# Inverting the 16x16 diagonal blocks of the recurrent chunks elementwise on VectorE, by way of DRAM, in place of eight TensorE products per pair of heads; the end of the group norm moved into the chain

## The reference, cut to what matters

```
def step(state, inp):
    r_t, w_t, k_t, v_t, aa_t, bb_t = inp
    sa = jnp.einsum('bhvk,bhk->bhv', state, aa_t)
    state = state * w_t[:, :, None, :] + sa[..., None] * bb_t[:, :, None, :] + v_t[..., None] * k_t[:, :, None, :]
    return state, jnp.einsum('bhvk,bhk->bhv', state, r_t)
...
mean = jnp.mean(y, axis=-1, keepdims=True)
var = jnp.mean(jnp.square(y - mean), axis=-1, keepdims=True)
y = ((y - mean) * lax.rsqrt(var + GN_EPS)).reshape(b, s, c) * lnx_w + lnx_b
...
return ((y + bonus) * g).astype(z.dtype)
```

## Time and profile before

| | |
|---|---|
| median of 3 runs | 2084.71 us (2084.33 to 2094.32) |
| profiled execution, its own time | 2084.17 us |
| its span | 2082.4 us |
| TensorE busy | 97% of the span |
| VectorE, ScalarE, GpSimd busy | 57%, 26%, 53% |
| mean granted TensorE clock | 0.987 of full |
| pair preparation and chains | from about 1134 to 1603 us |
| period of one pair in the steady part | 61.2 us |

### The profile page before, as it was taken

The page is one execution under the profiler, slowest core; times in us unless marked ns, Lnnn a source line. Parts: engine busy times, 40 slices in busy tenths (PEclk is TensorE's granted clock), DMA queues, the critical chain, the costliest instruction groups (busy, mean ns, idle before and its releaser), DMA issues.

```text
span 2082.4 us, 39410 instructions
## 1 busy us (share of the span) xinstructions
PE 2028.2 (97%) x16109; PEld 1675.5 (80%) x16109; DVE 1194.7 (57%) x1533; ACT 535.9 (26%) x1139; POOL 1106.9 (53%) x859
## 2 busy tenths in 40 slices
PE   8999999999999999999999999999999999999998
PEld 6888787877877787788877888888886878888886
DVE  6888724366767654212069677667673755665413
ACT  2100002233434212313143133332223023333101
POOL 6777764533533464544547044423365656666663
PEclk9999999999999998999999999999999999999999
DMA  4333231253453421312323022111213422332231
GB/s 136 102 102 102 91 101 54 82 176 122 130 157 114 150 81 61 101 49 74 124 56 93 14 66 66 40 53 49 63 62 127 136 97 81 101 101 88 89 112 56
DMA packets 181241, 190.27 MB, mean 91 GB/s; under 512 B 8525, under 2 KB 162268, under 8 KB 180828
## 3 DMA queue, kind: packets, MB, share of 16 engines
q1 hardware_dynamic: 172288, 181.81, 27.5%
q10 hardware_dynamic: 8796, 6.21, 1.0%
HBM read 179.56 MB, written 8.44 MB: 90 GB/s over the span
## 4 chain that ended last, share of the span: by engine, by line
PE 60%; DVE 4%; POOL 1%; issue 1%; DVEq 1%; POOLq 1%; ACT 1%; ACTq 0%
PE bank L900 8%; PE bank L902 8%; PE bank L901 8%; PE bank L1567 6%; PE bank L1528 3%; PE bank L1380 3%; PE bank L1396 2%; PE bank L1398 2%; PE bank L1397 2%; PE bank L1665 1%; PE bank L1302 1%; PE bank L1304 1%; PE bank L1303 1%; PE bank L1055 1%; PE bank L1269 1%
## 5 line engine op out<-in xcount | busy, mean ns | idle before, releaser
L738 POOL TENSOR_TENSOR wlo<-raws,whi 128x1024 fp32r<-128x1024 f32 (+5 forms) x312 | 677.6, 2172 | 46.6 <-issue 4.4
L736 POOL TENSOR_SCALAR whi<-raws 128x1024 fp32r<-128x1024 f32 (+5 forms) x312 | 332.2, 1065 | 308.3 <-PE bank L1057 172.9
L900 PE MATMUL bank<-hbuf,whi 128*128 128x512 f32 (+2 forms) x840 | 328.9, 392 | 0.0
L902 PE MATMUL bank<-hbuf,wlo 128*128 128x512 f32 (+2 forms) x840 | 327.7, 390 | 0.0
L901 PE MATMUL bank<-hbuf,whi 128*128 128x512 f32 (+2 forms) x776 | 302.7, 390 | 0.0
L649 POOL TENSOR_TENSOR spare<-ones 1x1 f32<-1x1 f32 x92 | 22.6, 246 | 347.1 <-PE bank L902 243.0
L900 PEld LDWEIGHTS bank<-hbuf,whi 128*128 128x128 f32 (+2 forms) x840 | 157.0, 187 | 35.2 <-POOL wlo L738 1.1
L902 PEld LDWEIGHTS bank<-hbuf,wlo 128*128 128x128 f32 (+2 forms) x840 | 156.9, 187 | 34.1
L901 PEld LDWEIGHTS bank<-hbuf,whi 128*128 128x128 f32 (+2 forms) x776 | 145.1, 187 | 31.3
L672 POOL TENSOR_SCALAR lg2L<-lg 128x128 fp32r<-128x128 f32 x8 | 2.4, 300 | 223.6 <-DMA lg<-in_g 223.6
L2650 DVE TENSOR_REDUCE nmax<-bank 128x4 f32<-128x512 f32 (+3 forms) x40 | 21.1, 550 | 146.0 <-PE bank L1277 104.2
(11 more groups left out here) (534 smaller groups left out, 4708.6 us busy)
## 6 DMA issues: line engine op xcount, KB each, us to landing
adaw<-in_w_ada SPq DMA_DIRECT2D x64, 384.0 KB, 4.1
raws<-in_w_up SPq DMA_DIRECT2D x22, 1024.0 KB, 4.9
raws<-in_w_in SPq DMA_DIRECT2D x41, 512.0 KB, 3.8
raws<-in_w_in SPq DMA_DIRECT2D x18, 1024.0 KB, 5.0
raws<-in_pool_w_in SPq DMA_DIRECT2D x16, 1024.0 KB, 5.4
raws<-in_mla_w_in SPq DMA_DIRECT2D x10, 1024.0 KB, 6.5
raws<-in_pool_w_out SPq DMA_DIRECT2D x8, 1024.0 KB, 4.9
raws<-in_mla_w_out SPq DMA_DIRECT2D x8, 1024.0 KB, 5.0
```

The lines of the kernel that those rows point to most:

```text
L736: G.tensor_scalar(h_, r_, 1.0, 1.0, ALU.mult, ALU.mult)
L738: G.tensor_tensor(l_, r_, f32(h_), ALU.subtract).then_inc(raw_split, 1)
L900: M.matmul(dst, wh, acts[k][0], start=(first and k == 0), stop=False)
L902: mm = M.matmul(dst, wl, acts[k][0], start=False, stop=(last and k == n - 1))
```

## The change

Levels 0 to 4 and the copy at level 5 go. In their place:

- TensorE computes the Gram matrix D already inside `gates(q)`, after 18 of the 48 products (`D_AFTER`), as soon as `bT` exists (`rk.ab`). The preparation is left with 12 products, in steps 1, 2, 4, 5, 7, 8, 10, 14, 16, 17, 19 and 21.
- DVE masks D and folds the four diagonal blocks of each chunk into a tile of 128x128 (`diagonal_blocks`). ACT writes it to DRAM in pieces of 16 floats (1024 of them) and, once that has landed, reads it back as 64 partitions of 1 KB, one 16x16 block each (`blocks_gathered`, between the two turns of `take_gates`).
- DVE inverts the 64 blocks with multiplications and sums along the free axis (`inverted_blocks`, 16 instructions and a transposing copy), at the start of `prepared(q)`.
- ACT writes block and transpose to DRAM after chunk 0 of the chain (`blocks_kept`, 128 pieces of 1 KB), waiting for `blk.x`, and reads them back after chunk 1 in pieces of 16 floats (2048) (`blocks_spread`). DVE spreads both over the diagonal (`spread_blocks`), before step 14.
- `finished(q-2)` moves from DVE's `wide_part` into `prepared(q)`: its reciprocal ahead of `inverted_blocks`, its three passes behind the taking of ak. `take_product(q, 2, ...)` moves behind `decayed_keys`.

```
 LEVELS = (
-    (("DA", "D", "N2"), ("D", "DA", "A2")),
-    (("N2", "A2", "A4"), ("A2", "U", "U")),
-    (("A4", "U", "V"),),
-    (("A4", "V", "V"),),
-    (("A4", "V", "V"),),
-    (("V", "I", "W"), ("E16", "V", "Z")),
+    (("E16", "V", "Z"),),
     (("W", "Z", "V"), ("Z", "W", "W")),
     (("E32", "V", "Z"),),
     (("W", "Z", "last"),),
 )
...
+D_AFTER = 18
...
             def gates(q):
...
-                for n in range(3 * DT):
+                for n in range(D_AFTER):
                     gate_part(q, n)
-                pe.wait_ge(sem("rk.bonus"), q)
-                pe.wait_ge(sem("rk.y"), q)
+                gram(q, "D")
+                for n in range(D_AFTER, 3 * DT):
+                    gate_part(q, n)
+                pe.wait_ge(sem("rk.sig"), q + 1)
...
                 if name == "D":
-                    pe.wait_ge(sem("rk.kr"), q + 1)
+                    pe.wait_ge(sem("rk.ab"), q + 1)
...
                 elif name == "qb":
-                    pe.wait_ge(sem("rk.ge"), q * 8 + GRAM_TAKEN["E32"])
+                    pe.wait_ge(sem("rk.kr"), q + 1)
+                    pe.wait_ge(sem("rk.ge"), q * 5 + GRAM_TAKEN["E32"])
                 elif name == "qk":
-                    pe.wait_ge(sem("rk.te"), q * 3 + 2)
...
+                    pe.wait_ge(sem("rk.te"), q * 3 + 3)
...
+            def blocks_gathered(q):
+
+                act.wait_ge(sem("blk.d"), q + 1)
+                act.dma_start(blocks_in[q % 2].rearrange("(c p j) -> p c j", c=CHUNKS, p=P),
+                              diagonal.rearrange("p (c j) -> p c j", c=CHUNKS)).then_inc(sem("blk.kept"), 16)
+                act.wait_ge(sem("blk.kept"), 16 * (q + 1))
+                act.dma_start(blk, blocks_in[q % 2].rearrange("(n x) -> n x", n=64)).then_inc(sem("blk.in"), 16)
+
+            def blocks_kept(q):
+
+                act.wait_ge(sem("blk.x"), q + 1)
+                act.dma_start(blocks_out[q % 2].rearrange("(w n x) -> n w x", w=2, n=64),
+                              hf[0:64, 0:2 * BLK * BLK].rearrange("n (w x) -> n w x", w=2)).then_inc(sem("blk.out"), 16)
+
+            def blocks_spread(q):
+
+                act.wait_ge(sem("blk.out"), 16 * (q + 1))
+                act.dma_start(hf[:, S + P:S + 3 * P].rearrange("p (x j) -> p x j", j=BLK),
+                              blocks_out[q % 2].rearrange("(x p j) -> p x j", p=P, j=BLK)).then_inc(sem("blk.back"), 16)
+
             def take_gates(q):
 
                 take_gate(q, 0)
+                if q >= 2:
+                    blocks_gathered(q)
                 take_gate(q, 1)
...
+                    if p + 1 < PAIRS and c < 2:
+                        (blocks_kept, blocks_spread)[c](p + 1)
...
-                if q >= 2:
+                if q == PAIRS:
+                    deviations(q - 2)
                     finished(q - 2)
-                if more:
+                if q == 1:
                     take_product(q, 2, vT[q % 2])
 
             def prepared(q):
...
-                gram("D")
-                taken(inv_D, 1, "up16")
+                if q >= 2:
+                    deviations(q - 2)
+                if q == 0:
+                    key_directions(1)
+                inverted_blocks(q)
                 gram("A")
-                taken(inv_DA, 0, "low16")
...
                 taken(inv_E16, 0, "step16")
                 taken(inv_E32, 0, "step32")
                 gram("ak")
                 taken(Gak, 7, "up1")
...
+                if q >= 2:
+                    finished(q - 2)
                 gram("qb")
                 taken(Gqb[q % 2], 0, "up0")
-                take_level(2)
+                take_turned(vtok, 7, "rk.tv")
+                take_turned(kN, 0, "rk.tk")
                 take_turned(bN[q % 2], 7, "rk.tb")
...
+                dve.wait_ge(sem("blk.back"), 16 * (q + 1))
+                spread_blocks(V, inv_D, blk_v).then_inc(sem("inv.v"), 1)
+                spread_blocks(V, tile(hf, 0), blk_w).then_inc(sem("inv.w"), 1)
...
+            def diagonal_blocks(q):
+
+                dve.wait_ge(sem("rk.block"), q + 1)
+                masked(inv_D, bank[1], "up16")
+                dve.drain()
+                V.tensor_reduce(diagonal.rearrange("p (c j) -> p c j", c=CHUNKS),
+                                inv_D[:, :].rearrange("p (c b j) -> p c j b", c=CHUNKS, j=BLK), AX.X, ALU.add)\
+                    .then_inc(sem("blk.d"), 1)
...
+            def inverted_blocks(q):
+
+                dve.wait_ge(sem("blk.in"), 16 * (q + 1))
+                V.memset(blk[:, 0:BLK * BLK:BLK + 1], 1.0)
...
+                for m in (4, 8):
+                    n, cube = BLK // (2 * m), [64, m, m, m]
...
+                    def times(lefts, rights):
+                        for b in range(n):
+                            terms = blk_terms[:, b * m ** 3:(b + 1) * m ** 3]
+                            V.tensor_tensor(terms.rearrange("n (i j k) -> n i j k", i=m, j=m),
+                                            lefts[b].unsqueeze(2).to_broadcast(cube),
+                                            rights[b].rearrange("n k j -> n j k").unsqueeze(1).to_broadcast(cube),
+                                            ALU.mult)
+                        dve.drain()
...
                 if p + 2 < PAIRS:
                     key_directions(p + 2)
                     decayed_keys(p + 2)
-                    dve.drain()
+                    take_product(p + 2, 2, vT[p % 2])
+                    diagonal_blocks(p + 2)
```

More of the change, by code:

```diff
@@ L193 @@
 )
-ADDED = {1: {"U": "U"}, 2: {"V": "U"}, 3: {"V": "U"}, 4: {"V": "U"}, 6: {"V": "V", "W": "W"}, 8: {"last": "V"}}
-GRAM_TAKEN = {name: n + 1 for n, name in enumerate(("D", "DA", "U", "E16", "E32", "ak", "qb", "qk"))}
-GRAM_MADE = {name: n + 1 for n, name in enumerate(("D", "A", "ak", "qb", "qk"))}
+ADDED = {1: {"V": "V", "W": "W"}, 3: {"last": "V"}}
+GRAM_TAKEN = {name: n + 1 for n, name in enumerate(("E16", "E32", "ak", "qb", "qk"))}
+GRAM_MADE = {name: n + 1 for n, name in enumerate(("A", "ak", "qb", "qk"))}
+BLK = 16
 def levels_taken(k):
@@ L384, in build @@
                     inverse = [tile(xT, 6), tile(xT, 7)]
-                    inv_t = {"D": inv_D, "V": inv_D, "DA": inv_DA, "A4": inv_DA, "U": inv_U, "E16": inv_E16,
-                             "E32": inv_E32, "N2": tile(hf, 0), "W": tile(hf, 0), "A2": tile(hf, 1), "Z": tile(hf, 1)}
-                    gn_x, gn_y, gn_sq, gn_dev = inv_DA, inv_U, inv_E16, inv_E32
+                    inv_t = {"V": inv_D, "E16": inv_E16, "E32": inv_E32, "W": tile(hf, 0), "Z": tile(hf, 1)}
+                    gn_y, gn_dev, gn_sq = inv_DA, inv_U, inv_E16
+                    blk, blk_t = hf[0:64, 0:BLK * BLK], hf[0:64, BLK * BLK:2 * BLK * BLK]
+                    blk_terms, blk_half = inv_D[0:64, :], hf[0:64, S + 3 * P:S + 3 * P + 64]
+                    diagonal, blk_v, blk_w = [hf[:, S + n * P:S + (n + 1) * P] for n in range(3)]
         with ExitStack() as st:
@@ L1593, in level @@
                 left, right, _ = LEVELS[k][w]
-                if k == 0 and w == 0:
-                    pe.wait_ge(sem("rk.ge"), q * 8 + GRAM_TAKEN["DA"])
-                elif k == 0:
+                if k == 0:
+                    pe.wait_ge(sem("inv.v"), q + 1)
+                    pe.wait_ge(sem("rk.ge"), q * 5 + GRAM_TAKEN["E16"])
+                elif k == 1 and w == 0:
+                    pe.wait_ge(sem("inv.w"), q + 1)
+                    pe.wait_ge(sem("inv.dve"), q * TAKEN_ALL + levels_taken(1))
+                elif k == 1:
@@ L1655, in started @@
+                elif step == 10:
+                    gram(q, "qk")
+                elif step == 14:
+                    level(q, 0, 0)
+                elif step == 16:
+                    level(q, 1, 0)
+                elif step == 17:
+                    level(q, 1, 1)
+                elif step == 19:
+                    level(q, 2, 0)
+                elif step == 21:
+                    level(q, 3, 0)
             def started(b, left, right, hi=CHUNKS):
@@ L1734, in _ @@
                     gate_part(1, n)
+            gram(1, "D")
             for p in range(PAIRS):
@@ L2256, in _ @@
             key_lengths(1)
-            take_gates(1)
+            blocks_gathered(0)
+            take_gate(1, 0)
+            blocks_kept(0)
+            blocks_spread(0)
+            take_gate(1, 1)
+            blocks_gathered(1)
             for p in range(PAIRS):
@@ L2791, in finished @@
                 dve.drain()
+            def finished(p):
+                x, pc = gn_y, pcol[p % 3]
                 V.scalar_tensor_tensor(x[:, :], gn_y[:, :], pc[:, 8:9], gn_dev[:, :], ALU.mult, ALU.mult)
```

129 lines of the change are left out of this document (65 added, 64 removed).

## The result

The changed kernel takes 2149.57 us (median of 4 runs, 2148.91 to 2154.15), the kernel before beside it 2085.84 (2084.33 to 2094.32). The ratio is 1.0291, 95% interval 1.0261 to 1.0321: slower by 2.9%. The profiled execution took 2154.15 us, its span is 2152.4, and 70.0 us longer than that of before. The page answers to the earlier trace rows: 17 us less of TensorE's busy time, in a span 70 us longer.

The account below looks back on a forecast made before the run. TensorE, 97% busy, was taken to bound the kernel. Six rounds +24, round q = 1 +3, first pair +7 and clock +12 made +46 us on 2084.17: 2130 us, range 2062 to 2165, likeliest case 2105 to 2160.

Parts of the forecast that it names:

- Wait for D: In the gates, TensorE waits for bT because VectorE's passes alternate with GpSimd's splits: 2.2 us per round.
- The inversion: VectorE's inversion of the blocks, from the read back to blk.x: 5.8 us, bounds 4.3 and 7.5.
- The stall in chunk 1: After chunk 0 ACT waits for blk.x, so TensorE gets chunk 1's right side 4.6 us late per steady round.
- the waits foreseen at steps 4, 7 and 10: In the chain, TensorE waits for VectorE's passes behind the inversion: 0.85, 0.6 and 0.25 us.
- The saving: In the chain, nine steps emptied of products save 5.24 us per round, and shorter level waits 1.1.
- level waits: TensorE's waits for the copies of levels, 1.55 us per round, shrink to some 0.45: gain 1.1.
- The first pair: First preparation: step 4 waits for the inversion, then transfers and `decayed_keys(1)` delay the first chain by 7 us.
- The clock: TensorE's gaps before D and in chunk 1 lower the granted clock: 1.7 us per round, +12 in seven rounds.
- A: Rival: no alternation and an inversion of 4.3 us, so chunk 0 covers it; 2054 us, chance 0.13.
- B: Rival, nearly even: no alternation but 5.8 us of inversion, stalls of 1 to 4 us; 2065 to 2090 us, chance 0.18.
- C: Rival: the emptier chain is granted 1.2 GHz throughout, some 10 us more per round; 2188 us, chance 0.07.
- D: Rival: the change doesn't do what it says; eight products fewer are not worth 7.4 us a round; no chance stated.

Follow-up runs that it names:

- experiment 2: Changed kernel with the second half of each GpSimd weight split left out in the recurrent phase: 2108.39 us (one run).
- Experiment 5: Changed kernel with all four transfers of pairs 2 to 6, and some of pairs 1 and 7, issued from SyncE's queue: 2150.10 us, ratio 1.0273.
- Experiment 6: Changed kernel with transfers on SyncE's queue, A and ak taken before the inversion, D after 30 gate products, steps and levels moved: 2131.91 us, ratio 1.0194.
- Experiment 7: Changed kernel without the four transfers and the inversion, the folded blocks spread as they are: 2088.89 us, ratio 0.9984.
- experiment 1: Changed kernel with D computed after 30 of the 48 gate products in place of 18: 2152.73 us, ratio 1.0303.
- experiment 10: Changed kernel without transfers and inversion, and with D after 30 gate products in place of 18: 2079.85 us, ratio 0.9934.
- experiment 8: Changed kernel with the second pair's gate products 20 to 47 at step 3 of the first preparation: 2145.71 us (one run).
- 11: Changed kernel with the edits of Experiment 6 and experiment 8, and qb made at step 3 and taken before the inversion: 2143.14 us, ratio 1.0222.
- experiment 4: Changed kernel with five useless products added at step 3 of each chain from the second on, where TensorE waits: 2144.51 us, ratio 1.0266.

## Why the prediction came out as it did

The direction and the mechanism were right, and 2149.57 lies in the range and in the likeliest case; the size was 20 us short. In the profiled executions, where +46 stood against +70.0, the miss is 13.5 us in the first pair, 9.2 in the seven rounds (+48.2, where 24 + 3 + 12 stood) and 1.3 behind the last chain. By its own steps:

**Wait for D.** Foreseen 2.2 us from the alternation of VectorE and GpSimd; measured 2.19. The Trainium skill's rule (SBUF — State Buffer, Who interferes with whom) and the trace agree: 2.03 us beside the splits, 0.69 without them in experiment 2. The rest is 4.5 us longer (40.56 against 36.08), where the terms gave 3.15 (the wait, and 0.95 for ACT) and the clock. The sum has the wait in seven rounds, though only six hold a D among their gates; it came in five, since in the sixth GpSimd was done in time.

**The inversion.** 6.74 us, not 5.8: the multiplications over 512 elements took 1.01 and not 0.69 (one factor is repeated and the other read across rows; which of the two makes it slower no run shows). It was within the bounds. `blk.x` came 10.2 us after the end of the gates (1466.19), where 10.8 stood. The transfers: the first write 2.2 (2.4 foreseen), the read with its way to VectorE 2.7 from its issue (2.1). The prediction takes 2 us of fixed cost from the Trainium skill (DMA: Bandwidth & Descriptors, Anatomy of one DMA), whose section gives them for transfers that GpSimd issues; these are ACT's, and landed in 2.2 and 2.1 us (medians of 8).

**The stall in chunk 1.** 5.80 us where 4.6 stood; the waits foreseen at steps 4, 7 and 10 (1.7 in all) came to almost nothing, since ACT's wait already covered them. Without the trip the chain takes 21.60, with it 28.28: 6.7 us with the lower clock in it, where the waits alone were foreseen at 6.3. Experiment 5 shows that two queues held the same wait, VectorE's behind ACT's: removing one alone gives nothing. Experiment 6, which freed both, gave 18 us together with its other edits.

**The saving, the step that was mis-sized.** For the chain the prediction had eight of the nine emptied steps, 4.31, and 1.1 of level waits: 5.4 us. Experiment 7 gives 3.6. The three gaps without a filler are 0.82, 0.64 and 0.65: emptying a step is worth 0.46, 0.53 or 0.40, near the estimate, and the eight of them (two, five and one) 4.0. The level waits were read wrongly: of the 12.4 us in 8 rounds, 6.6 lie in the first preparation and 0.6 in a steady chain (whose whole idle time of TensorE is 0.39 by the windows, which count otherwise). So at most 0.6 of the 1.1 could be gained there. Why 3.6 was measured, a little under the sum of the steps, is open. One group of the first preparation alone has 3.2:

```profile
L1567 PE MATMUL bank<-hf 64*64 64x64 f32 x128 | 4.4, 220 | 3.2 <-DVE hf L2843 3.2
```

**Two terms on one path.** The sum took the chain's start behind the wait for D, and the wait for the block from there, which holds. But 2.2 us is not the price of that wait: experiment 1 removes that wait and gains nothing, experiment 10 removes it where no trip follows and gains 9 us.

**The first pair.** +20.5, not +7, the largest miss. TensorE waited three times in it:

```profile
1142.37 1.97 PE L1571 MATMUL bank<-bT,aT 64*64 64x64 f32 x32 [6.69 <-DVE Rr L2752]
...
1157.96 1.98 PE L1571 MATMUL bank<-rT,bT 64*64 64x64 f32 x32 [6.72 <-DVE inv_E L2734]
...
1179.77 3.68 PE L1571 MATMUL bank<-hf 64*64 64x64 f32 x64 [6.20 <-DVE hf L2869]
```

Only the second was named. Ahead of step 1 stand passes of VectorE for the second pair, drawn out by the splits; ahead of the levels `decayed_keys(1)`, which was named and thought to be covered.

The first of these waits is there in some executions and not in others. The changed kernel and experiment 8 have the same code up to that place. In the one a copy of 8 elements on each partition fell beside a split of GpSimd (1133.54 to 1136.60), in the other, which came there 2.3 us earlier, between two splits:

```profile
1134.53 2.09 DVE L2769 COPY mid<-cc 128x8 f32<-128x8 f32 x1
...
1132.27 0.17 DVE L2769 COPY mid<-cc 128x8 f32<-128x8 f32 x1
```

Several passes around it fare alike, and the wait is 6.69 us in the one and 0.23 in the other. In the profiled execution of the kernel before this copy took 0.17. Experiments 7 and 10 have the same first preparation too, the one with the wait and the other without: their first chains start at 1178.91 and 1173.72. So the 20.5 divide like this: 13.4 for the trip (1192.33 against 1178.91, both with the wait), 5.2 for how VectorE and GpSimd happened to meet, 1.9 for all else. The 5.2 are not the change's in every execution. The prediction's +7 is short by the trip above all.

**The seventh chain.** +7.2; by the prediction's terms for a chain (-5.24, -1.1 and 6.3 of waits) nothing and the clock. There GpSimd splits beside the chain, and the inversion runs from 1600.53 to 1613.6, 13.1 us, twice its time; its 512-element multiplications take 1.68 and 1.94. The prediction had the rule and priced it in the gates and the first preparation alone. Experiments 6 and 11 made this worse (50.2 and 53.3 us).

**The clock.** Predicted 1.7 us a round; the gate products behind D alone lose 1.58, and experiment 4 gives some 1.0 more back in the chain. Two of TensorE's gaps a round, one of 2.2 us and one of 5.8, were each followed by windows of less than 1.00, in part of 0.50 (1.2 GHz), as shown above. The Trainium skill (TensorE: Matmul & The Clock Gate, Part 1) says the same, that idleness halves the clock; what it costs is taken from these rows.

**The rivals.** A, the inversion in time, asked for the block within 6 us of the chain's start; it came after 10. B asked for no alternation: experiment 2 makes that true and still gives 2108, above B's 2065 to 2090. C, a low clock through whole chains, did not come: 0.88 in the mean of the chain. D was nearer the truth than it was given: eight products fewer are worth 0.7% at most.

## What to carry to other kernels

Before a product is taken out of a chain of dependent steps, measure what the chain costs without any filler: here eight of 0.93 us were worth 3.6 us, and the wait and the clock around the moved product cost 4 us elsewhere. A long trip (here 17.6 us over four transfers and VectorE) has to be hidden in every queue that waits for it, each of which serves others too; freeing one queue only shows the next. A sum of waits taken over a phase is no price per round: read it in the window of one round. And before two profiles are subtracted, look where their executions differ apart from the change: here 5 us of 70 lay in passes that met another engine in the one and missed it in the other.

## What the runs showed of the hardware that was not expected

- A multiplication on 64 partitions over 512 elements, with one factor broadcast and one read across rows, took 1.01 us, the sum over as many 0.68, and a plain pass over 128 partitions and 512 elements 0.69.
- A small dependent pass (8 elements on 64 partitions) took 0.16 us and the next began 0.24 after it began; beside GpSimd's splits the same one took up to 1.11, and the inversion of 17 such and larger instructions 13.1 us in place of 6.74.
- A copy of 8 elements on 128 partitions took 0.17 us between two splits and 2.09 us beside one. Whether VectorE came there 2 us earlier or later moved the first chain by 5 us.
- Useless products in a gap made the kernel faster: 5 us less in all (four runs of 2142.09 to 2146.08 against four of 2148.91 to 2154.15), and the clock stayed at 1.00.
